# Latent mixer of a four-layer block: projections in another order, scores two heads ahead, rotated parts of two heads in one tile, head norms taken from PSUM

## The reference

```python
proj = h @ mla_w_in[j]                                   # h: 256 x 1024
q = (_rmsnorm(c_q, q_a_norm) @ w_q_b).reshape(B, S, MLA_HEADS, MLA_NOPE + MLA_ROPE)
kv = (_rmsnorm(c_kv, kv_a_norm) @ w_kv_b).reshape(B, S, MLA_HEADS, MLA_NOPE + MLA_V)
q_nope = _rmsnorm(q[..., :MLA_NOPE], q_norm[:MLA_NOPE])
q_pe = _apply_axial_rope(_rmsnorm(q[..., MLA_NOPE:], q_norm[MLA_NOPE:]), rope)
k_nope = _rmsnorm(kv[..., :MLA_NOPE], k_norm[:MLA_NOPE])
v = kv[..., MLA_NOPE:]
k_pe = _apply_axial_rope(_rmsnorm(k_pe, k_norm[MLA_NOPE:])[:, :, None, :], rope)[:, :, 0, :]
out = _blocked_attention([q_nope, q_pe], [k_nope, k_pe], v, (MLA_NOPE + MLA_ROPE) ** -0.5)
mem_out = _memory_attention(q_mem, mem_n, w_mem_kv[i], memq_norm[i], memk_norm[i])
x = x + jnp.concatenate([mix, mem_out], axis=-1) @ w_out[i]
```

## Time and profile before

| | us |
|---|---|
| median of three runs | 1319.05 |
| profiled execution | 1323.42 |
| its span, first to last instruction | 1321.6 |
| TensorE busy (matmul) | 1268.4 |
| VectorE busy | 811.4 |
| ScalarE busy | 686.0 |
| GpSimd busy | 87.2 |
| mean granted TensorE clock, share of full | 0.986 |

### The profile page before, as it was taken

One profiled execution on the slowest core, in us unless ns is written; L12 is line 12 of the kernel. 1 busy time (PEld: TensorE's weight loads), 2 busy tenths in 40 slices (PEclk: granted clock), 3 DMA queues, 4 the chain that ended last, 5 costly groups with the idle time before them and its releaser, 6 DMA issues.

```text
span 1321.6 us, 15913 instructions
## 1 busy us (share of the span) xinstructions
PE 1268.4 (96%) x6374; PEld 1039.1 (79%) x6374; DVE 811.4 (61%) x1048; ACT 686.0 (52%) x1086; POOL 87.2 (7%) x112
## 2 busy tenths in 40 slices
PE   6999999999987999999998899999999999999998
PEld 4777888887876788888887668888887888888886
DVE  7985666645876666664566543666545784656652
ACT  7655644434687664443578723644434763644431
POOL 2410000000000100000122100000000300000000
PEclk9999999999998899999999999999999999999999
DMA  7234555554633455555555203555554523555551
GB/s 287 97 101 140 180 193 185 189 191 164 235 131 129 154 198 179 184 187 191 173 183 191 94 3 128 189 180 178 188 189 171 192 79 114 191 181 180 183 188 63
DMA packets 32393, 216.61 MB, mean 164 GB/s; under 512 B 3888, under 2 KB 4272, under 8 KB 7232
## 3 DMA queue, kind: packets, MB, share of 16 engines
q1 hardware_dynamic: 30240, 210.19, 45.7%
q0 software_dynamic: 1360, 4.78, 1.1%
q10 hardware_dynamic: 720, 0.63, 0.1%
HBM read 214.54 MB, written 1.05 MB: 163 GB/s over the span
## 4 chain that ended last, share of the span: by engine, by line
PE 77%; DVE 11%; ACT 7%; issue 3%; POOL 1%; DMA 1%; SPq 0%; DVEq 0%; ACTq 0%
PE PS L417 21%; PE PS L419 21%; PE PS L418 21%; PE PS L423 4%; DVE WL L1671 3%; ACT WH L1074 2%; PE PS L454 2%; PE PS L457 2%; PE PS L455 2%; PE PS L687 1%; ACT JK L1110 1%; ACT HTh L1091 1%; PE PS L710 1%; DVE YG L1939 1%; DMA RAW<-in_w 1%
## 5 line engine op out<-in xcount | busy, mean ns | idle before, releaser
L1671 DVE TENSOR_TENSOR WL<-RAW,WH 128x2048 fp32r<-128x2048 f32 (+2 forms) x200 | 443.3, 2222 | 355.6 <-ACT WH L1074 355.5
L1074 ACT ACTIVATE WH<-RAW 128x2048 fp32r<-128x2048 f32 (+2 forms) x200 | 371.1, 1860 | 394.6 <-PE PS L419 393.3
L417 PE MATMUL PS<-WH,HTh 128*128 128x512 f32 (+1 forms) x880 | 349.8, 397 | 10.8 <-DVE WL L1671 8.8
L419 PE MATMUL PS<-WH,HTl 128*128 128x512 f32 (+1 forms) x880 | 343.3, 390 | 0.0
L418 PE MATMUL PS<-WL,HTh 128*128 128x512 f32 (+1 forms) x880 | 342.9, 390 | 0.0
L417 PEld LDWEIGHTS PS<-WH,HTh 128*128 128x128 f32 x880 | 166.7, 189 | 46.5 <-DVE WL L1671 10.9
L419 PEld LDWEIGHTS PS<-WH,HTl 128*128 128x128 f32 x880 | 166.6, 189 | 35.1
L418 PEld LDWEIGHTS PS<-WL,HTh 128*128 128x128 f32 x880 | 167.0, 190 | 32.3
L417 PE MATMUL PS<-WH,YAh 128*128 128x512 f32 x386 | 153.8, 398 | 2.5 <-DVE YAl L1687 1.1
L418 PE MATMUL PS<-WL,YAh 128*128 128x512 f32 x386 | 151.2, 392 | 0.0
L419 PE MATMUL PS<-WH,YAl 128*128 128x512 f32 x386 | 151.2, 392 | 0.0
(11 more groups left out here) (354 smaller groups left out, 1483.0 us busy)
## 6 DMA issues: line engine op xcount, KB each, us to landing
RAW<-in_w SPq DMA_DIRECT2D x196, 1024.0 KB, 4.9
BC<-in_rows POOLq DMA_DIRECT2D x4, 512.0 KB, 4.0
YG<-in_mem POOLq DMA_DIRECT2D x4, 512.0 KB, 4.9
X<-in_x SPq DMA_DIRECT2D x2, 512.0 KB, 6.3
RAW<-in_w SPq DMA_DIRECT2D x4, 256.0 KB, 5.7
BC<-in_s SPq DMA_DIRECT2D x1, 512.0 KB, 11.0
BB<-in_s SPq DMA_DIRECT2D x1, 512.0 KB, 11.5
YG<-in_s SPq DMA_DIRECT2D x1, 512.0 KB, 12.3
```

The lines of the kernel that those rows point to most:

```text
L417: e.matmul(out, ah, bh, start=start, stop=False)
L419: return e.matmul(out, al, bh, start=False, stop=stop)
L1074: e.activation(WH[:, c % NW, w], RAW[:, c % NR, w], ACT.Copy).then_inc(S.hi, 1)
L1671: e.tensor_tensor(WL[:, c % NW, w], RAW[:, c % NR, w], WH[:, c % NW, w].bitcast(f32), SUB).then_inc(S.lo, 1)
```

## The change

Five things change in the third mixer; the rest of the program is the same.

1. Order of the weight chunks and products: `mla_a`, `mla_b`, `mla_c`, `qb0`, `kvb0`, `qb2`, `mem10`, `mem11`, `qb1`, `kvb1`, `out0`, where it was `mla_a`, `mla_b`, `mla_c`, `mem10`, `qb2`, `mem11`, `qb0`, `kvb0`, `qb1`, `kvb1`, `out0`. `qb1` and `kvb1` now stand before the attention. Turns are placed inside products (`at={k: ...}`), not between them. The memory rows are turned inside `qb0`.
2. Attention by `attention_ahead`, in head order latent 0 to 3, memory 0 to 3, latent 4 to 7. The last group's turn goes behind the first chunk of `out0`, whose row tiles are taken in the order 0, 2, 8, 10, 4, 6 (pairs).
3. The rotated query parts of two heads lie in one tile of 128 rows (`QTp` 128 x 4 x 256, 8 transposes); the rotated key lies twice in `KPT` 128 x 2 x 256, once in the upper and once in the lower 64 rows, with zeros in the others. So the second product of a latent head also runs over 128 rows. GpSimd fills `KPT` with zeros first. `rope` writes the key's part a second time (`twin`).
4. Queries and keys without rotation are not evacuated before their norm: ScalarE squares both banks in one instruction from PSUM (`all_squares`), VectorE sums per head (`head_sum`, one reduction of 128 x 1024), and scales from PSUM into the Z buffer (`scaled_out`).
5. The norms of memory queries, rotated queries and memory keys take the same wide square and reduction, from the Z buffer.

```diff
-            QTp = sb("QTp", [64, 8, 256])
-            KPT = sb("KPT", [64, 256])
+            QTp = sb("QTp", [128, 4, 256])
+            KPT = sb("KPT", [128, 2, 256])
...
+            return dict(parts=[(QTn[:, h, :], KTn[:, h, :]), (QTp[:, h // 2, :], KPT[:, h % 2, :])],
...
             edge_mm(PLAN["mla_a"], 4, 448, (0, 1), 4)
             rows_mm(PLAN["mla_b"], 8, 8, 256, HT, (2, 3))
-            mem_rows(1)
-            rows_mm(PLAN["mla_c"], 4, 8, 512, HT, (0, 1), evacuated("za"))
-            e.wait_ge(S.z, ZEV["zb"] + 2)
-            c_turn((0, 1), 2)
-            c_turn((2, 3), 3)
-            rows_mm(PLAN["mem10"], 4, 8, 512, HT, (0, 1), mem10_ready)
...
+            rows_mm(PLAN["mla_c"], 4, 8, 512, HT, (0, 1), evacuated("za"),
+                    at={2: [lambda: c_turn((0, 1), 4)], 4: [lambda: c_turn((2, 3), 5)], 5: [lambda: c_turn((4,), 6), turn_kp]})
+            rows_mm(PLAN["qb0"], 3, 3, 512, CQ, (2, 3), qb0_ready,
+                    at={0: [lambda: mem_rows(1, mem_free, (0, 1))], 1: [lambda: mem_rows(1, mem_free, (2, 3))]})
+            rows_mm(PLAN["kvb0"], 2, 2, 512, CK, (6, 7), kvb0_ready, keep=S.kv)
+            rows_mm(PLAN["kvb0"], 2, 2, 512, CK, (0, 1), evacuated("zc"), off=1024)
+            rows_mm(PLAN["qb2"], 3, 3, 512, CQ, (4, 5), qb2_free)
+            rows_mm(PLAN["mem10"], 4, 8, 512, HT, (0, 1), mem10_ready,
+                    at={1: [lambda: gain_turn(ZD, "n0", (2, 3))], 3: [lambda: gain_turn(ZA, "nk0", (6, 7))],
+                        5: [lambda: gain_turn(ZC, "zm", (4, 5), lambda jp: e.wait_ge(S.z, ZEV["z2"] + jp + 1))]})
+            rows_mm(PLAN["mem11"], 4, 8, 512, HT, (2, 3), copied("qt0"),
+                    at={3: [lambda: gain_turn(ZB, "qp", (4, 5), lambda jp: e.wait_ge(S.gout, GT["qmt"] + jp + 1))],
+                        6: [lambda: gain_turn(ZC, "memk1", (0, 1))]})
+            rows_mm(PLAN["qb1"], 3, 3, 512, CQ, (6, 7), copied("kt0"))
+            rows_mm(PLAN["kvb1"], 2, 2, 512, CK, (4, 5), copied("qpt"), keep=S.kv)
+            rows_mm(PLAN["kvb1"], 2, 2, 512, CK, (2, 3), vm_out, off=1024, at={0: [lambda: products2(0)], 1: [lambda: products2(1)]})
+            attend2()
+            wide_mm(PLAN["out0"], 5, lambda k: (YAh, YAl, OUT0[k // 2] + k % 2), lambda ci: e.wait_ge(S.ol, 3 + ci), lambda: finish2(8))
...
+            def fill2(h):
+                if h == 2:
+                    gain_turn(ZD, "n1", (4, 5), lambda jp: e.wait_ge(S.nz, NZ["nk1"] + 2))
+                elif h == 4:
+                    gain_turn(ZA, "nk1", (4, 5), lambda jp: e.wait_ge(S.gout, GT["qt1"] + jp + 1))
+
+            def pvfree2(h):
+                if h == 0:
+                    e.wait_ge(S.nz, NZ["n1"] + 2)
...
+            def all_squares(out, src, d):
+
+                e.activation(out, src, ACT.Square, scale=d ** -0.5).then_inc(S.hsq, 1)
...
+            copy(KPT[0:64, 0, :], PS[0:64, 7, 0:256])
+            copy(KPT[64:128, 1, :], PS[64:128, 7, 0:256]).then_inc(S.kpt, 1)
...
+            def head_sum(name, sq, d):
+                n = 1024 // d
+                e.wait_ge(S.hsq, HSQ[name] + 1)
+                e.tensor_reduce(st[:, SO[name]:SO[name] + n], sq.rearrange("p a (h d) -> p (a h) d", d=d), AX.X, ADD).then_inc(S.hsum, 1)
+
+            def scaled_out(name, Z, bks):
+
+                e.wait_ge(S.rs, RSTD[name])
+                for t in range(2):
+                    r = st[:, SO[name] + 4 * t:SO[name] + 4 * t + 4]
+                    e.tensor_tensor(Z[:, t, :].rearrange("p (h d) -> p h d", d=128), PS[:, bks[t], :].rearrange("p (h d) -> p h d", d=128),
+                                    r.unsqueeze(2).to_broadcast([128, 4, 128]), MUL).then_inc(S.nz, 1)
...
+            def fill2(h):
+                if h == 0:
+                    head_sum("nk1", ZA[:, :, :], 128)
+                    scaled_out("n1", ZD, (6, 7))
+                elif h == 1:
+                    scaled_out("nk1", ZA, (4, 5))
+                    feed(PLAN["mem11"][1])
+                elif h == 3:
+                    feed(PLAN["qb1"][0])
+                elif h == 7:
+                    feed(PLAN["kvb1"][0])
...
+            e.memset(KPT[:, :, :], 0.0).then_inc(S.fills, 1)
```

More of the change, by code:

```diff
@@ L677, in attention0, with attention_ahead @@
                 finish(1)
-            def attention(base, heads, P, PT, Y, ready, fill, tfree, pvfree):
+            def attention_ahead(base, heads, P, PT, Y, ready, fill, pvfree, tfree=None):
                 def products(h):
@@ L732, in attention_ahead @@
[L732 to L748 removed]
+                    elif tfree:
+                        tfree()
@@ L1555, in act @@
-            feed(PLAN["qb0"][0])
-            z_evac("zk0", None, (0, 1), ZC, kv=1)
-            e.wait_ge(S.qpr, 1)
-            head_norm("n0", two(ZA), 4, 128, "z0")
-            e.wait_ge(S.hsq, HSQ["n0"] + 8)
-            head_norm("nk0", two(ZC), 4, 128, "zk0")
-            for h2 in range(4):
-                e.wait_ge(S.qpp, h2 + 1)
-                copy(QTp[:, 2 * h2:2 * h2 + 2, :], PS[0:64, 4 + h2, :].rearrange("p (a c) -> p a c", a=2)).then_inc(S.qpt, 1)
-            z_evac("vt0", PLAN["kvb0"][0], (2, 3), VV[:, :, 0:512])
@@ L1565, in act, with attn_group, attention_ahead @@
-            feed(PLAN["kvb0"][0])
-            gain_turn("qt0", lambda j: QTn[:, j:j + 2, :], gq[:, 0:1], (4, 5))
-            gain_turn("kt0", lambda j: KTn[:, j:j + 2, :], col("mla_kn"), (6, 7))
-            def attention(base, heads, P, M, den, fill):
-                def scores(h):
+            def attn_group(base, heads, g, at):
+                for jp in range(2):
+                    attn_out(2 + 2 * ((base - 8) // 4 + g) + jp + 1, heads[4 * g]["banks"][jp], at + 2 * jp)
+            def attention_ahead(base, heads, P, M, den, fill, at):
+                for h in range(12):
@@ new lines, in act @@
+            feed(PLAN["mla_c"][0])
+            z_evac("zc", PLAN["mla_c"][1], (0, 1), ZC, 512, True)
+            mem_hi(1)
+            feed(PLAN["mla_c"][1])
+            e.wait_ge(S.used, PLAN["qb0"][0] + 1)
+            all_squares(ZD[:, :, :], PS[:, 2:4, :], 128)
+            feed(PLAN["qb0"][0])
+            e.wait_ge(S.kv, 1)
+            all_squares(ZA[:, :, :], PS[:, 6:8, :], 128)
+            z_evac("vt0", PLAN["kvb0"][0], (0, 1), VV[:, :, 0:512])
+            e.wait_ge(S.msq, 4)
+            all_squares(JK2, ZC[:, :, :], 128)
@@ new lines, in dve @@
+            roped[0] = dv.n
+            e.tensor_scalar(gq[:, 0:1], col("mla_qn"), sc_mla, None, MUL)
+            e.tensor_scalar(gq[:, 1:2], col("memq_norm_2", 0), sc_mem, None, MUL).then_inc(S.gq, 1)
+            c_norm("zq", ZA, 384)
+            feed(PLAN["mla_a"][1])
+            for t in range(2):
+                rope("pe", ZA[:, t, 384:448], 1, 64, t, tg[:, 1, :, :, :], RP, RQ, ZA[:, t, 448:512])
+            c_norm("zk", ZB, 256)
+            feed(PLAN["mla_b"][0])
+            c_lo(1, (0, 1), 4)
@@ new lines, in dve @@
+            c_lo(2, (2, 3), 5)
+            c_lo(3, (4,), 6)
+            feed(PLAN["mla_c"][0])
+            mem_lo(1)
+            feed(PLAN["mla_c"][1])
+            head_sum("n0", ZD[:, :, :], 128)
+            feed(PLAN["qb0"][0])
+            head_sum("nk0", ZA[:, :, :], 128)
+            scaled_out("n0", ZD, (2, 3))
+            head_sum("zm", JK2, 128)
+            scaled_out("nk0", ZA, (6, 7))
+            feed(PLAN["kvb0"][0])
+            head_sum("qp", JK2, 64)
+            scaled("zm", two(ZC), 4, 128)
@@ new lines, in dve @@
+            feed(PLAN["qb2"][0])
+            for t in range(2):
+                rope("qp", ZB[:, t, :], 8, 64, t, tg[:, 0, :, :, :], RP, RQ)
+            feed(PLAN["mem10"][0])
+            head_sum("memk1", JK2, 128)
+            feed(PLAN["mem10"][1])
+            scaled("memk1", two(ZC), 4, 128)
+            feed(PLAN["mem11"][0])
+            head_sum("n1", ZD[:, :, :], 128)
+            def fill2(h):
+                if h == 0:
+                    head_sum("nk1", ZA[:, :, :], 128)
+                    scaled_out("n1", ZD, (6, 7))
+                elif h == 1:
+                    scaled_out("nk1", ZA, (4, 5))
+                    feed(PLAN["mem11"][1])
+                elif h == 3:
+                    feed(PLAN["qb1"][0])
+                elif h == 7:
+                    feed(PLAN["kvb1"][0])
```

495 lines of the change are left out of this document (173 added, 322 removed).

## The result

The kernel after takes 1295.75 us (median of four runs, 1294.96 to 1297.76), the kernel before 1319.37 (four runs, 1318.75 to 1322.88). The ratio is 0.982 (95% interval 0.981 to 0.983): 23.6 us less. The forecast was 1294.0 us. The profiled execution took 1297.76 us, its span is 1296.0 at a mean granted clock of 0.991; before it was 1321.6 at 0.986.

The account below looks back on a forecast made before the run. TensorE bounds the kernel: 129.1 us of stretch hold 108.0 of work. Work of 108.0 - 5.9 - 0.8 = 101.3 plus 2.7 of waits gives 104.0, 25.1 less, so median 1294.0 us; range 1291.3 to 1298, to 1303 with A and B.

Parts of the forecast that it names:

- Rival A: Latent heads' scores: any second part costs 0.63, so 128 rows gain nothing; 1294.0 + 5.9 = 1300 us; chance 0.10.
- Rival B: `kvb0` or first heads: VectorE or ScalarE 2 us late, TensorE pauses, clock may fall; two places 7 us, 1301; chance 0.20.
- The 5.9 us for the scores over 128 rows: Eight latent heads: scores 1.72 instead of 2.40 us, turn 0.43 instead of 0.49, 8 x 0.74 = 5.9 us less.
- The order of the projections: Projections: every turn stands at least one product behind its norm, so 6.5 of 11.7 us of waits go.
- the forecast one at `kvb0`: `kvb0`, memory rows' eight pieces: ScalarE and VectorE need 3.2 us, so TensorE waits 0.2 us.
- the root of eight heads: Norms in the projections: the root of eight heads was put at 2.0 us, 1.67 of it the power.
- The first `pv`: Attention start: VectorE does `head_sum` and `scaled_out` first, so TensorE waits from 736.6 to 737.8, 1.2 us.
- The 0.3 us forecast for head 2: Attention: `feed` at h = 1 puts a 2.2 us split ahead of head 2's copy; TensorE waits 0.3 us.
- The 3.3 us for the divided group: Attention: TensorE's wait for the divided group before each turn, 3.3 us, goes.
- The 1.9 us for the copied probabilities: Attention: TensorE's wait for the copied probabilities, 1.9 us, goes.
- Rival C: Latent attention: clock falls to 1.2 GHz at `pv(0)` until `out0`, +33 - 25 = +8 us, 1327; chance 0.03.
- Rival D: Third mixer: removed waits were covered by others, only TensorE's own work falls, 6.7 us, 1312; chance 0.05.

Follow-up runs that it names:

- the 64-row experiment: Kernel after with the second product of a latent head over 64 rows again: 1302.29 us, ratio 0.9876, stretch 108.91 us against 103.8.
- the grouped run: Kernel after with 64-row second products, a head's products of one height placed side by side: 1299.25 us, ratio 0.9849, stretch 106.15 us.
- the experiment of order and norms: Kernel after with three things put back, 64-row second products, scores one head ahead, finished group turned at once: 1305.18 us, ratio 0.9891, stretch 111.94 us.
- the group's turn at once: Kernel after with a finished group's turn directly behind its last values, not behind the next head's: 1300.75 us, ratio 0.9861, stretch 107.81 us.
- the pause put in: Kernel after with TensorE waiting before `mem10` for a ScalarE square it does not need: 1302.71 us, ratio 0.9872, stretch 108.12 us.
- The version with the norms early: Kernel after with VectorE's norms of second keys and queries moved ahead of the first row maximum: 1293.22 us, ratio 0.9809, stretch 101.90 us.
- the kernel before with wide scores: Kernel before with both rotated tiles filled with zeros to 128 rows, all else kept: 1317.43 us, ratio 0.9992; again 1318.27 us, 0.9993.

## Why the prediction was right or wrong

The forecast said 1294.0, with a range of its own of 1291.3 to 1298, up to 1303 with rivals A and B; the median is 1295.75. Its mechanism, mostly, and its size were right, with these points.

**The work of TensorE: right in the heads.** A latent head was put at 3.05 us and takes 3.05. The 5.9 us for the scores over 128 rows, which no row of before showed, is what the rows of the 64-row experiment give back, 0.75 for each head. Rival A (any second part costs 0.63) fell: with 128 rows the second part starts 0.43 behind the first. The Trainium skill, "TensorE: Matmul & The Clock Gate", section "Why this matters for your kernels", lets a matmul over few rows take as long as one over 128, by which the step would be worth 0. That holds here for products of one height side by side; where the heights alternate the runs disagree (0.63 against 0.43). The Trainium skill, "TensorEngine Tiling (Array Packing)", section "Key Properties", has the engine drained at a change of the tiling mode; the grouped run fits a cost at each change, 2.02 against 2.40 us with half the changes; no run shows the drain itself.

**The order of the projections: right for TensorE.** It was the walk through the five lists that was at risk here. It put TensorE at `mem10` at 692.7, `mem11` at 706.4, the first score at 727.5 and ready for the first `pv` at 736.6, counted from 664.5; the stretch began 1.24 us earlier, which makes 691.5, 705.2, 726.3 and 735.4. Measured are 691.75, 705.35, 726.57 and 735.73, the end of the turn ahead of that `pv`. The only wait of this part is the forecast one at `kvb0`, 0.3 where 0.2 was written. What the experiment of order and norms leaves in carries 17.2 of the 25.3 us, with the 0.9 that only moved and up to 1.6 that may be before's scatter; taking the norms from PSUM is 0.7 of it, and the clock's 5.3 us are among it. Rival B (pauses in another place) did not come in any window.

One duration of the walk was wrong, and a margin hid it. It had the root of eight heads at 2.0 us. In the kernel after, GpSimd needs 4.0 us for that of the first queries (687.05 to 691.02): 1.67 for the power as written, but 2.22 for the small operation ahead of it, which runs at the same time as VectorE's split (686.87 to 689.15); the next one, at 691.11 with no split beside it, takes 0.25. So these queries were scaled some 0.9 us later than written (692.3 instead of 691.4). Their turn came at 694.48, and nothing waited.

**The first `pv`: right.** A wait of 1.2 us on VectorE's scaling of Z was forecast, and it is the 1.2 in TensorE's waits above, in front of the `pv` at 737.08.

The 0.3 us forecast for head 2 is no row of its own among the waits. The values of head 2 start 0.71 us behind the turn of four ahead of them, where it is 0.44 in the latent head shown above, so 0.27 us may be lost there.

**The attention's waits: sum right, one reason wrong.** The 3.3 us for the divided group go with the later `finish`, as written: put back, they are 3.1. The 1.9 us for the copied probabilities were put down to the serial order, and scores two heads ahead were to remove them. That step failed. With scores one head ahead no turn waits for copied probabilities, nor in the run with one ahead and the group's turn at once; with the late queries and keys turned in the probabilities' banks they wait again, 5.4 us. The trace of before, read turn by turn, shows 1.7 of its 1.9 us in front of those late turns, so it could have been seen ahead. The sentence gave two waits to one edit without asking which bank each waits for. That the sum came out all the same was luck: the new kernel happened to turn these queries and keys in other banks, a part of the edit that the prediction did not price.

**The parts as a sum: only in the new order.** The prediction priced each edit by itself. The wide scores are worth 5.1 us in the kernel after and 1.6 of the attention in the kernel before (against its one profile), where the whole kernel shows nothing. A reader who had made that edit first would have thrown it away.

**Rival C, the slow clock through the attention: it didn't come.** The wait of 1.2 us at the first `pv` was followed by a clock of 1.00; where the clock did fall, it was for some 3 us at half speed behind the pause put in and some 6 in the window at 0.71 (2.9 us lost), never for 25. **Rival D** is refuted by the medians, 23.6 us apart where it gave 6.7.

**The mis-sized terms.** The stretch was to be 103.1 us (104.0 less the 0.9 inside `out0`) and is 103.8. The version with the norms early tells where the 0.7 lies. It takes 101.9 with 0.3 of wait, against 100.4 of work alone in the forecast (101.3 - 0.9): so 1.2 us can't be placed, for the 1.0 written. The waits at the first `pv` and at head 2 cost 1.9 instead of 1.5, since the instructions behind them start slower, and the one at `kvb0` 0.3 instead of 0.2.

The larger error is the way from profile to median. The stretch took 0.7 us more than forecast, but it began 1.2 us earlier, so the profiled execution, put at 1298.3, took 1297.8. From there I subtracted 4.4 us, the distance of before's profiled execution from its median; for the kernel after it is 2.0. These 2.4 us, less the 0.5 by which the profiled execution was shorter, are, but for rounding, the 1.75 us between forecast and median. The 4.4 was no property of profiling but one execution's scatter: in the 14 profiles the start of the stretch alone moves by 4.4 us.

## What to carry to other kernels

Walk each engine's list by hand with durations of the trace before: here it gave TensorE's times to 0.3 us, and the margins at the turns took up an error of 0.9 in another engine's. Price a pause of TensorE by its length and the slow clock that may follow, and an edit that shortens TensorE's work by what the other engines have to cover afterwards; in a tight serial order it may return nothing until the order is changed. When a wait vanishes with several edits at once, ask which buffer it was for: the trace before often names the instruction that waited. Keep matmuls of one height next to each other. And profile the kernel before more than once when its stretches are to be compared.

## What the runs showed of the hardware

- A change between products over 128 and over 64 rows costs about 0.19 us, and the 64-row product saves nothing: four f32 products of 256 columns take 1.72 us over 128 rows, 2.02 with the 64-row ones side by side, and 2.40 alternating.
- Length alone does not tell whether the 1.2 GHz level follows a pause. Pauses of 2.8 and 3.3 us were followed by it, in the first case for nearly 3 us (1.5 us lost). One of 2.2 us (the late turns in the probabilities' banks), one of 1.2 (first `pv`) and two of 1.3 (the group's turn at once) were not: the granted clock is 1.00 in the windows around them. The same pause of 1.8 us was followed by 0.51 in before and by 1.00 in the kernel before with wide scores. There, pauses of up to 1.5 us close together, in a window in which TensorE was busy for 6.91 of 10 us, were followed by a window at 0.71, and by one at 0.70 in its second profile.
- A small GpSimd operation (128x8) took 2.22 us beside VectorE's split and 0.25 without one.
- The whole kernel's time moves by some 4 us between executions. In the 14 profiles the stretch starts between 660.2 and 664.6 us, while what follows it repeats to 0.1 us in the kernel before and its variants (527.9 to 528.0) and to 0.4 us in the kernel after and its own (528.7 to 529.1). An edit worth 1 or 2 us shows in the length of its stretch, which repeated to 0.04 us in the two pairs of profiles, and hardly in five runs of the whole.
